# Row stage with operand sums made among the column pairs, the raw product last, and the next weight blocks split early

## The reference, cut to what matters

```python
hn = rmsnorm(h, norm_ffn)
g, up = jnp.split(hn @ w_ffn_in, 2, axis=-1)          # 22 tiles of 128 hidden features
h = h + (jax.nn.silu(g) * up) @ w_ffn_out             # D_FF = 2816 rows
x = rmsnorm(h, norm_final)                            # then the second block:
u = x @ w_in                                          # gates, q, k, v, ... of the mLSTM
```

## Time and profile before

| | |
|---|---|
| median of 3 runs | 3338.17 us (3336.87 to 3340.07) |
| the profiled execution | 3340.51 us, its span 3338.4 us |
| TensorE | 3194.8 us busy (96%), granted clock 0.989 of full speed |
| VectorE, ScalarE, GpSimd | 59%, 35%, 49% busy |
| column pairs | 760 to 1141 us of the span |
| row stage | 1157 to 1373 us |

### The profile page before, as it was taken

One profiled execution on the slowest core, in us unless ns is written; L12 is line 12 of the kernel. 1 busy time (PEld: TensorE's weight loads), 2 busy tenths in 40 slices (PEclk: granted clock), 3 DMA queues, 4 the chain that ended last, 5 costly groups with the idle time before them and its releaser, 6 DMA issues.

```text
span 3338.4 us, 41113 instructions
## 1 busy us (share of the span) xinstructions
PE 3194.8 (96%) x15258; PEld 2532.7 (76%) x15258; DVE 1973.4 (59%) x2372; ACT 1152.1 (35%) x1893; POOL 1632.6 (49%) x975
## 2 busy tenths in 40 slices
PE   8999999989999999889999899999999989999997
PEld 6776678768888778778876678888888858767775
DVE  6325645785333488797866673333333468988735
ACT  5435511043333334433323352222222341333351
POOL 5771134438888755413322147676676743333332
PEclk9999999999999999999999999999999999999998
DMA  3232014112222463131111121111111211111111
GB/s 120 104 116 69 34 49 182 49 33 76 85 84 82 154 212 101 46 95 58 64 37 35 37 82 60 41 60 52 50 58 43 89 51 39 43 43 50 42 32 70
DMA packets 72042, 236.11 MB, mean 71 GB/s; under 512 B 7792, under 2 KB 8432, under 8 KB 70896
## 3 DMA queue, kind: packets, MB, share of 16 engines
q1 hardware_dynamic: 54800, 162.03, 15.2%
q10 hardware_dynamic: 17120, 72.40, 5.8%
HBM read 203.46 MB, written 30.94 MB: 70 GB/s over the span
## 4 chain that ended last, share of the span: by engine, by line
PE 74%; DVE 13%; issue 4%; ACT 4%; POOL 3%; DMA 2%; ACTq 0%; DVEq 0%; POOLq 0%; SPq 0%
PE acc L1587 26%; PE acc L503 24%; PE acc L1603 7%; PE acc L523 5%; PE acc L1650 3%; PE acc L971 2%; PE acc L945 2%; POOL w_lo L3569 1%; DVE conv_slots L3127 1%; PE acc L595 1%; PE acc L545 1%; PE acc L922 1%; POOL raw L3564 1%; ACT band_probs L1086 1%; DVE h L1137 1%
## 5 line engine op out<-in xcount | busy, mean ns | idle before, releaser
L3554 POOL TENSOR_TENSOR w_hi<-raw,zero 128x1024 fp32r<-128x1024 f32 x107 | 219.0, 2047 | 1155.5 <-PE acc L503 551.5
L3569 POOL TENSOR_TENSOR w_lo<-raw,w_hi 128x512 fp32r<-128x512 f32 x318 | 488.5, 1551 | 206.3 <-ACT w_hi L1685 206.0
L1137 DVE TENSOR_TENSOR h<-h,acc 128x1024 f32<-128x1024 f32 x240 | 292.5, 1221 | 163.6 <-PE acc L1603 120.7
L3558 POOL TENSOR_TENSOR w_lo<-raw,w_hi 128x1024 fp32r<-128x1024 f32 x114 | 320.7, 2813 | 105.0 <-ACT w_hi L2522 96.6
L1685 ACT ACTIVATE w_hi<-raw 128x512 fp32r<-128x512 f32 x318 | 191.0, 625 | 410.4 <-POOL raw L3564 148.9
L1587 PE MATMUL acc<-x_hi,w_hi 128*128 128x512 f32 x812 | 316.3, 390 | 4.0 <-POOL w_lo L3569 1.4
L1587 PE MATMUL acc<-x_hi,w_lo 128*128 128x512 f32 x812 | 316.0, 389 | 0.0
L1587 PE MATMUL acc<-x_lo,w_hi 128*128 128x512 f32 x812 | 316.0, 389 | 0.0
L3564 POOL TENSOR_TENSOR raw<-raw 128x512 f32<-128x512 f32 x159 | 241.6, 1520 | 68.8 <-DMA raw<-blocks 58.5
L503 PE MATMUL acc<-x_hi,w_hi 128*128 128x512 f32 x816 | 257.0, 396 | 16.4 <-POOL w_lo L3558 4.5
L1587 PE MATMUL acc<-t_hi,w_hi 128*128 128x512 f32 x672 | 262.3, 390 | 3.4 <-POOL w_lo L3569 2.3
(11 more groups left out here) (498 smaller groups left out, 6824.7 us busy)
## 6 DMA issues: line engine op xcount, KB each, us to landing
raw<-blocks SPq DMA_DIRECT2D x189, 512.0 KB, 3.6
raw<-blocks SPq DMA_DIRECT2D x106, 256.0 KB, 2.6
raw<-row_pieces SPq DMA_DIRECT2D x22, 512.0 KB, 3.5
piece_block<-row_pieces SPq DMA_DIRECT2D x22, 512.0 KB, 3.5
hid_dram<-act_g ACTq DMA_DIRECT2D x11, 512.0 KB, 2.6
hid_dram<-act_h ACTq DMA_DIRECT2D x10, 512.0 KB, 2.6
h<-x_t ACTq DMA_DIRECT2D x8, 512.0 KB, 8.8
h<-x_t ACTq DMA_DIRECT2D x2, 2048.0 KB, 13.2
```

The lines of the kernel that those rows point to most:

```text
L1137: dve.tensor_tensor(h[:, j, :], h[:, j, :], acc[s], ALU.add).then_inc(acc_free[s], 1)
L3554: pool.tensor_tensor(hi, raw[:, slot, :], nothing, ALU.add).then_inc(hi_split, 1)
L3558: pool.tensor_tensor(lo, raw[:, slot, :], hi.bitcast(F32), ALU.subtract).then_inc(w_split, 1)
L3569: pool.tensor_tensor(half_tile_range(w_lo, at_), halves(source), half_tile_range(w_hi, at_).bitcast(F32), ALU.subtract).then_inc(half_spli ...
```

## The change

- VectorE makes the four sums of the hidden tiles that the row products need (odd_high - even_high, that + even_low, even_high - even_low, odd_low - the second) behind every second pair (`sum_hidden`); ScalarE stores 7 half tiles (act_g, act_h, hidden_sums) with three DMAs once for two pairs, behind a wait for `hid_summed`; the last is stored by SyncE. The row stage has no `sum_part` any more and reads one 128x512 part for each step from `hid_dram` into a ring of eight.
- The order of steps is products 0 to 4, parts 0 to 2 of product 5, all of product 6, and the rest of product 5 (its weights and operand are not sums); the last three steps are run together, output tile by output tile. TensorE waits at the end for 24 additions and not for 28.
- The two weight blocks behind the stage are loaded, rounded and lowered at steps 36/42 and 50/56 into buffers of their own (first_stage, first_hi, first_lo); the two next are loaded behind the last pieces and rounded by ScalarE before it waits for the mean. `release_next` and GpSimd's split of the first two go. The mean is asked for behind tile KT - 4 and not KT - 2. One row of h is scaled in front of gate_rows and not three.

```diff
+ROW_ORDER = [(i, part) for i, first, after in ((0, 0, ROW_PARTS), (1, 0, ROW_PARTS), (2, 0, ROW_PARTS), (3, 0, ROW_PARTS),
+                                               (4, 0, ROW_PARTS), (5, 0, 3), (6, 0, ROW_PARTS), (5, 3, ROW_PARTS))
+             for part in range(first, after)]
...
+            row_steps(pe, range(ROW_STEPS - ROWS_TOGETHER, ROW_STEPS))
+            pe.wait_ge(rows_added, FEATURE_PAIRS * (PRODUCTS - 1))
+
+        def row_steps(pe, steps):
+            for m in range(FEATURE_PAIRS):
+                for step in steps:
+                    i, part = ROW_ORDER[step]
+                    if m == 0:
+                        pe.wait_ge(row_split, step + 1)
+                        pe.wait_ge(part_made, step + 1)
...
+            def store(part):
+                act.wait_ge(hid_summed, t.next("hid_summed"))
+                for out, (source, first, after) in zip(hid_out, hidden_parts):
+                    act.dma_start(hid_dram[:, bass.ds(part, 1), first:after, :].rearrange("p a b n -> p (a b) n"), source)\
+                       .then_inc(out, 16)
...
             def pair(b, follow, stored, behind_snap=None):
                 def store_last():
-                    if stored is not None:
-                        store(stored, 1 - b)
                     if behind_snap is not None:
                         behind_snap()
+                    if stored is not None:
+                        store(stored)
...
-                pair(0, "pair", 2 * n + 3)
-                pair(1, "pair", 2 * n + 4)
+                pair(0, "pair", n + 1)
+                pair(1, "pair", None)
...
+        def sum_hidden(dve, t, ch):
+            even_low, even_high = act_g[:, 0:HALF], act_g[:, HALF:TOK]
+            odd_low, odd_high = act_h[:, 0:HALF], act_h[:, HALF:TOK]
+            dve.wait_ge(hid_made, t.count("hid_made"))
+            dve.wait_ge(hid_out[2], t.count("out2") * 16)
+            t.next("out2")
+            ch.link(dve.tensor_tensor(hidden_sums[:, 0, :], odd_high, even_high, ALU.subtract))
+            ch.sync()
+            ch.link(dve.tensor_tensor(hidden_sums[:, 1, :], hidden_sums[:, 0, :], even_low, ALU.add))
+            ch.link(dve.tensor_tensor(even_high, even_high, even_low, ALU.subtract))
+            ch.sync()
+            dve.tensor_tensor(hidden_sums[:, 2, :], odd_low, hidden_sums[:, 1, :], ALU.subtract).then_inc(hid_summed, 1)
...
-        def sum_part(dve, step):
-            i, part = divmod(step, ROW_PARTS)
-            if i not in SUMMED_PARTS:
-                return
-            low, high = even_low[part], even_high[part]
...
         def gates_tensor(pe, t):
-            release_next(pe)
             for _ in range(KT):
                 t.next("squared")
-            feature_pair(pe, t, expect_parts(t, KT), lambda: raw_mean(pe, t), KT - 2, True, ODD_FIRST)
+            feature_pair(pe, t, expect_parts(t, KT), lambda: raw_mean(pe, t), KT - 4, False, ODD_FIRST, (first_hi, first_lo))
...
+        def rounded_behind_rows(act, ch):
+            kept_gain(act, ch)
+            round_block(act, BEHIND_1 + 2, BEHIND_1 + 1)
+            round_block(act, BEHIND_1 + 3, BEHIND_1 + 1)
...
         def gates_vector(dve, t, ch):
             ch.link(dve.memset(before[:, :], 0.0))
-            scale_kept(dve, ch, 0, 3)
+            scale_kept(dve, ch, 0, 1)
             s = await_acc(dve, t)
             dve.tensor_tensor(gate_rows[:, :], acc[s], first_root[:, :], ALU.mult).then_inc(acc_free[s], 1)
-            scale_kept(dve, ch, 3, 4)
+            scale_kept(dve, ch, 1, 4)
...
             def load_row_stage(done):
...
+                sp.wait_ge(hid_summed, ROW_PARTS)
+                for out, (source, first, after) in zip(hid_out, hidden_parts):
+                    sp.dma_start(hid_dram[:, ROW_PARTS - 1, first:after, :], source).then_inc(out, 16)
+                for out in hid_out:
+                    sp.wait_ge(out, 16 * ROW_PARTS)
+                loaded = ROW_RING
+                for step in range(ROW_STEPS):
+                    while loaded < ROW_BLOCKS and behind_row_block(loaded - ROW_RING) == step + 1:
+                        sp.wait_ge(row_split, step + 1)
+                        load_pieces(loaded)
+                        loaded += 1
...
+                    if step + PART_RING < ROW_STEPS:
+                        sp.wait_ge(part_made, step + 1)
+                        load_part(step + PART_RING)
+                    if step in FIRST_LOADED:
+                        b = FIRST_LOADED.index(step)
+                        sp.wait_ge(w_split, BEHIND_1 + b - PLAIN_2)
+                        sp.dma_start(first_stage[:, :], blocks[BEHIND_1 + b]).then_inc(raw_in[b], 16)
...
+                    if step in FIRST_ROUNDED:
+                        b = FIRST_ROUNDED.index(step)
+                        pool.wait_ge(hi_split, BEHIND_1 + b + 1 - PLAIN_2)
+                        hi, lo = (w[:, b, :, :].rearrange("p a b -> p (a b)") for w in (first_hi, first_lo))
+                        pool.tensor_tensor(lo, first_stage[:, :], hi.bitcast(F32), ALU.subtract).then_inc(w_split, 1)
...
-            pool.wait_ge(step_used, ROW_STEPS - 1)
-            split_first(BEHIND_1, PLAIN_2, 2)
```

More of the change, by code:

```diff
@@ L531, in release_next, with feature_pair @@
             pe.matmul(acc_all[:, 2 * TOK:2 * TOK + P], mean_w[:, :], ident[:, :], start=True, stop=True).then_inc(w_used, 1)
-        def feature_pair(pe, t, parts_from, beside=None, behind=KT - 1, released=False, order=tuple(range(KT))):
+        def feature_pair(pe, t, parts_from, beside=None, behind=KT - 1, released=False, order=tuple(range(KT)),
+                         first=None):
             slots, accs = [], []
+            high, low = first or (w_hi, w_lo)
             def begin():
@@ L541, in tile_of @@
             def tile_of(b, k):
-                for m, (w, part) in enumerate(((w_hi, x_hi), (w_hi, x_lo), (w_lo, x_hi))):
+                for m, (w, part) in enumerate(((high, x_hi), (high, x_lo), (low, x_hi))):
                     for half in range(2):
@@ L1637, in rows_tensor @@
             await_all_taken(pe, t)
-            for step in range(ROW_STEPS):
-                i, part = divmod(step, ROW_PARTS)
+            for step in range(ROW_STEPS - ROWS_TOGETHER):
                 if step == ROW_PARTS:
@@ L2158, in mixed_ffn_vector @@
             pair_vector(dve, t, ch, 0)
             def first_parts():
-                lower_part(dve, 0)
-                lower_part(dve, 1)
+                for step in range(ROW_RING):
+                    lower_part(dve, step)
             pair_vector(dve, t, ch, 1, first_parts)
+            sum_hidden(dve, t, ch)
             ch.reset()
         def lower_part(dve, step):
-            i, part = divmod(step, ROW_PARTS)
             dve.wait_ge(part_high, step + 1)
-            dve.tensor_tensor(row_part_lo[step % ROW_RING], part_source(i, part), row_part_hi[step % ROW_RING].bitcast(F32),
+            dve.tensor_tensor(row_part_lo[step % ROW_RING], part_at(step), row_part_hi[step % ROW_RING].bitcast(F32),
@@ L3474, in load_behind_rows, with load_part @@
                 load(1 - p, n + 1)
-            hid_parts = hid_dram.rearrange("p (k two) n -> p two k n", two=2)
             def load_pieces(block):
-                if block >= ROW_RING:
-                    sp.wait_ge(row_split, behind_row_piece(2 * (block - ROW_RING) + 1))
                 sp.dma_start(piece_ring[block % ROW_RING], row_pieces[block]).then_inc(piece_in[block % ROW_RING], 16)
-            def load_parts(runs, run, first, after, odd, high, at_, landed):
-                sp.dma_start(runs[run][:, first:after, :],
-                             hid_parts[:, odd, at_:at_ + after - first, high * HALF:(high + 1) * HALF]).then_inc(landed, 16)
+            def load_part(step):
+                i, part = ROW_ORDER[step]
+                sp.dma_start(part_at(step), hid_dram[:, part, PART_SLOT[i], :]).then_inc(part_in[step % PART_RING], 16)
             def load_row_stage(done):
@@ L3504, in load_row_stage @@
[L3504 to L3516 removed]
+                for block in range(2, ROW_RING):
+                    load_pieces(block)
@@ new lines, in load_row_stage @@
+                sp.wait_ge(hid_summed, ROW_PARTS)
[9 more added lines that the diff above has]
+                        loaded += 1
+                    for slot in range(2):
+                        if behind_row_block(ROW_BLOCKS - ROW_RING + slot) == step + 1:
+                            sp.wait_ge(row_split, step + 1)
+                            load(slot, BEHIND_1 + 2 + slot)
+                    if step + PART_RING < ROW_STEPS:
[5 more added lines that the diff above has]
+                        sp.dma_start(first_stage[:, :], blocks[BEHIND_1 + b]).then_inc(raw_in[b], 16)
@@ L3819, in row_blocks_of @@
     quarters = (((0, 0),), ((0, 0), (1, 0)), ((1, 1),), ((1, 1),), ((0, 0),), ((0, 1),), ((0, 1),))
```

(2 more changed lines are left out.)

207 lines of the change are left out of this document (83 added, 124 removed).

## The result

The changed kernel takes 3373.75 us (median of 4 runs, 3373.14 to 3376.72), the kernel before beside it 3337.56 (4 runs, 3336.87 to 3340.07): ratio 1.0109, 95% interval 1.0091 to 1.0126, or 36.2 us more. 3362.8 had been predicted, in a range of 3336 to 3380.

| from ...

The account below looks back on a forecast made before the run. TensorE, busy 96% of the span, was taken as the bound. Nine pair repetitions 29.7, first store 6.0, row stage -2.6 and behind the rows -8.5 sum to +24.6 us on the median 3338.17: 3362.8, range 3336 to 3380.

Parts of the forecast that it names:

- hole, nine rounds: Column pairs with a store, steady state: TensorE stands 2.4 us in front of product 4, nine times.
- the clock or the next pair: Behind each hole in the pairs: either TensorE's clock falls or the next pair stalls; 0.9 us each, bounds 0 and 2.5.
- first store: First of the ten stores in the column pairs: product 4 is 4.3 us late, 6.0 us with the clock.
- row stage: VectorE's sums leave (-4.3), part 10's store (+0.7), last three steps wanting step 76's operands early (+1.0): -2.6 us.
- behind the rows: After the row stage: old hole and low clock go, a new hole of some 3 us at the mean; -8.5 us (-4 to -13).
- The sums take turns with GpSimd: Column pairs: each VectorE sum waits for the rest of a GpSimd operation plus 0.55 us; sums end at 1050.3, not 1045.8.
- Rival A: Column pairs: the sums fit without waiting in turn and the pairs lose nothing; 3321 to 3334 us, chance 0.13.
- the room: Column pairs: time for the sums after the multiply (1043.17), free until 1046, plus 1.7 us before TensorE stands.
- Three issues, 1.15 us: ScalarE's three DMA issues between the sums' wait and rounding 4, taken at 0.38 us each.
- The other moves in the pairs are free: Column pairs: stores growing to 1792 KB in two pairs, at a mean of 83 GB/s, are hidden under 38 us.
- rival D: Column pairs: every hole of 2.4 to 3.0 also costs clock and next pair; +47 us, 3380 to 3392, chance 0.07.
- C: The forecast case for the whole kernel: 3345 to 3380 us, chance 0.68.

Follow-up runs that it names:

- three_sums: Changed kernel with the third of the four sums left out, so one stored operand is another value; 3351.51 us, ratio 1.0035.
- one_sum: Changed kernel making and storing a single sum, which the row stage reads for all three; wait and three issues stay; 3322.61 us, ratio 0.9949.
- sums_beside_product_3: Changed kernel with sums in their own tile, started after product 2 and stored at the gate; act_g and act_h stored without a wait; 3323.26 us, ratio 0.9947.
- sums_at_old_place: sums_beside_product_3 without the wait for product 2's end, so the sums stand right behind the pair's last multiply; 3328.75 us, ratio 0.997.
- one_sum_stored: Changed kernel making all four sums but storing one hidden sum (256 KB in the third DMA, not 768); 3372.22 us, ratio 1.0099.
- clock_held: Changed kernel plus twelve matmuls into an unread bank in front of product 4 of nine pairs with a store; 3376.57 us, ratio 1.0106.
- store_late: Changed kernel with ScalarE's wait for hid_summed and its three stores moved behind the second snapshot, no longer before roundings 4 and 5; 3358.17 us, ratio 1.005.
- stores_beside_loads: sums_beside_product_3 with act_h and 1 MB that nobody reads stored behind the second snapshot, beside the next pair's load; 3343.31 us, ratio 1.0015.
- part_10_later: sums_beside_product_3 with SyncE's store of part 10 and its wait moved from before step 8's load to before step 10's; 3319.14 us, ratio 0.9941.

## Why the prediction was right, step by step

The direction, the place and the mechanism were right; +24.6 us had been summed and +36.2 measured. The terms of the pairs were too small by 20 us, and the gain behind the rows as well. That the time still lies within the range is in part luck: the larger gain behind the rows (3.5 to log_f, 5.7 in all) and 3.4 us in front of the pairs, which no edit explains, took back nearly half of those 20. By its own sign, a pairs' window 25 to 40 us longer, the prediction missed: it was 55.8.

| step | predicted | measured |
|---|---|---|
| hole, nine rounds | 2.4 each, 21.6 | 3.1 each, 27.8 |
| "the clock or the next pair" | 0.9 each, 8.1 | 2.35 each, 21.2 |
| first store | 6.0 | 6.8 (hole 5.05; the rest is what follows the tenth hole, by difference) |
| row stage | -2.6 | -1.3 |
| behind the rows | -8.5 | -12.0 to log_f, -14.2 in all |

- **The sums take turns with GpSimd: right.** 1.67 to 1.77 each, where the plain duration is 0.68, and done 6.8 us behind the multiply, where 7.1 had been worked out. The Trainium skill's rule ("SBUF — State Buffer", section "Who interferes with whom"), that a VectorE instruction with two SBUF inputs contends for one shared port pair, an exclusive lock, with a GpSimd instruction that reads SBUF, agrees with these rows. Rival A is out; three_sums and one_sum show besides that the cost begins where the sums outgrow the room.
- **ScalarE's order carries it: right**, and shown from the other side: with the same sums, as slow, but no rounding behind them, the pairs are as fast as before (sums_beside_product_3), and 7 us slower with the sums at their old place (sums_at_old_place).
- **Three issues, 1.15 us: too small.** They took 1.83, the third 0.84 at 768 and at 256 KB (one_sum_stored). That is the 0.7 by which the steady holes were mis-sized, and the first one.
- **"Bounds 0 and 2.5; I take 0.9": the step that missed most**, 13 of the 19 us that the nine rounds came out over the sum. Both of its causes were named, with a choice of the lesser cost. In the changed kernel's own rows 20.2 of the 21.2 us are matmuls at the low pace and 1.0 is a wait for a low half. clock_held shows that taking the clock's part away gains nothing, since the load-to-GpSimd chain then costs as much in the mean: the two are alternatives, of which the larger counts in each round. The slower load in that chain had not been foreseen.
- **"The other moves in the pairs are free": wrong as put.** The stores land on the load of the next pair: 5.2 us instead of 3.7 in the changed kernel, 7.6 in store_late, 7.1 in stores_beside_loads. How much of the 2.35 is this was not taken apart in the changed kernel, and stays open.
- **The case:** in the pairs it was rival D that came, 9 x 5.44 where D had 5.5, not C. That the time is below D's 3380 comes from 5.7 us more behind the rows and from the 3.4 in front of the pairs. "No hole to win" in the pairs missed one of 1.0 us in the kernel before (at 795.31), which the changed kernel does not have and which is taken off in the 6.8 of the first store.
- **Row stage:** VectorE's sums went and the middle holes with them, as said. Part 10's store cost more than 0.7: 0.9 in front of step 4, and 2.3 with some low clock in front of step 8. The 1.0 for step 76 did not come; the tile-by-tile end has no hole and is worth 3.4.
- **Behind the rows:** the hole of 3 at the mean was right (2.9), with the square sums ready at T + 14.0 where T + 14 was worked out, and gate_rows at T + 22.9 for T + 24 (that and T + 35.3 before are 1.3 of the missing 3.5 us). The rest, some 2.3, is the price of the kept scales, put at 2 to 4: from gate_rows to log_f it is 7.1 us instead of 6.7, so the kept scales fit beside what ScalarE does there. The 2.2 behind log_f had no term.

With the waits undone, the edits' own gains stand alone: of the 21.0 us by which part_10_later's span is shorter than that of before, 4.7 lie between the end of the pairs and the end of the rows, 12.1 from there to log_f and 1.7 behind it; 2.1 stand in front of the pairs, where the code is the same.

## What to carry to other kernels

Before work is put in front of a wait in an engine's order, list what stands behind that wait; with the same sums the kernel was 36 us slower than before where the roundings waited for them, and 17 us faster where nothing did. Where a late step starts two chains to the same engine, price both and take the larger, since curing one (here the clock) only uncovers the other. A mean bandwidth does not say that a transfer is hidden: look at what else is issued in the same few microseconds and who waits for it.

## What the runs showed of the hardware

- The third of three DMA issues in a row on ScalarE's queue takes 0.82 to 0.87 us in the steady rounds, the first two 0.34 to 0.36, at 768 KB (the changed kernel) and at 256 KB (one_sum_stored) alike. In three_sums (768 KB) and one_sum (256 KB), where the issues come earlier behind the multiply, it is 0.66 to 0.67. So the bytes do not set it; what does stays open. Two in a row (stores_beside_loads) took 0.35 and 0.45.
- Of two engines in turns both slow down, but not alike: VectorE's sum goes from 0.68 to 1.7 us, GpSimd's operation from 1.29 to 1.62 and 1.74, while in the wide operations both went to over 3.
- A 512 KB load beside 1.5 to 1.8 MB of stores issued in the 1.2 us before it took 7.1 to 7.6 us from its issue to the operation that waits for it, instead of 3.7 to 3.9.
